# Four feed-forward units of six by seven block products, two of their four weight sums made by accumulating DMA reads

## The reference

```python
D_MODEL, SEQ, D_FF = 1024, 256, 2816

def rmsnorm(x, g):
    return x * rsqrt(mean(x * x, axis=-1) + 1e-6) * g

def swiglu(x, w_gu, w_down):                   # w_gu: 1024 x 5632, w_down: 2816 x 1024
    gate, up = split(x @ w_gu, 2, axis=-1)
    return (silu(gate) * up) @ w_down

for i in range(4):
    x = x + 0.5 * swiglu(rmsnorm(x, ffn1_norm[i]), ffn1_w_gu[i], ffn1_w_down[i])
    x = x + mixer_i(rmsnorm(x, mix_norm[i]))    # attention, SSD, short convolution, attention
    x = x + 0.5 * swiglu(rmsnorm(x, ffn2_norm[i]), ffn2_w_gu[i], ffn2_w_down[i])
```

## Time and profile before

| | |
|---|---|
| median of three runs | 2102.91 us |
| profiled execution | 2101.92 us |
| its span, first to last instruction | 2100.2 us |
| mean granted TensorE clock | 0.995 |
| busy: PE, DVE, ACT, POOL | 98%, 72%, 53%, 4% |
| DMA: bytes moved, mean rate | 369.5 MB, 176 GB/s |
| one feed-forward, from 345.7 to 527.8 us | 182.1 us |

### The profile page before, as it was taken

The page is one execution under the profiler, slowest core; times in us unless marked ns, Lnnn a source line. Parts: engine busy times, 40 slices in busy tenths (PEclk is TensorE's granted clock), DMA queues, the critical chain, the costliest instruction groups (busy, mean ns, idle before and its releaser), DMA issues.

```text
span 2100.2 us, 25376 instructions
## 1 busy us (share of the span) xinstructions
PE 2061.0 (98%) x10493; PEld 1741.3 (83%) x10493; DVE 1503.2 (72%) x1431; ACT 1116.2 (53%) x1180; POOL 79.9 (4%) x110
## 2 busy tenths in 40 slices
PE   7999999999999999999999999999999999999998
PEld 5888887888888789988888888988888888988886
DVE  6885556885976568868776885779758776557884
ACT  5454555554654465655545554446545554556453
POOL 1000000000000002210000000000000000000000
PEclk9999999999999999999999999999999999999999
DMA  5755533655456384454575655565464665523751
GB/s 204 241 200 166 175 101 100 221 195 185 165 176 203 120 262 121 122 198 163 179 242 161 220 188 164 171 200 201 164 229 130 219 228 170 164 81 100 240 201 70
DMA packets 216838, 369.54 MB, mean 176 GB/s; under 512 B 9900, under 2 KB 92164, under 8 KB 216212
## 3 DMA queue, kind: packets, MB, share of 16 engines
q1 hardware_dynamic: 216020, 363.65, 52.5%
q0 software_dynamic: 704, 4.28, 0.5%
HBM read 366.81 MB, written 1.08 MB: 175 GB/s over the span
## 4 chain that ended last, share of the span: by engine, by line
PE 87%; DVE 5%; ACT 4%; POOL 1%; issue 1%; DMA 1%; SPq 0%; POOLq 0%; DVEq 0%; ACTq 0%
PE bank L1424 59%; PE bank L1545 14%; PE bank L1430 7%; ACT w_hi L645 2%; PE bank L1577 2%; DVE w_lo L996 2%; DVE arena L1295 2%; PE bank L1717 1%; PE bank L1709 1%; PE bank L1463 1%; DMA stage<-in_ssd_w_in 1%; POOL yms L579 0%; ACT arena L893 0%; PE bank L1710 0%; PE bank L1718 0%
## 5 line engine op out<-in xcount | busy, mean ns | idle before, releaser
L996 DVE TENSOR_TENSOR w_lo<-stage,w_hi 128x2048 fp32r<-128x2048 f32 (+1 forms) x248 | 560.8, 2264 | 231.5 <-ACT w_hi L645 230.6
L645 ACT ACTIVATE w_hi<-stage 128x2048 fp32r<-128x2048 f32 (+1 forms) x248 | 468.8, 1891 | 309.5 <-PE bank L1424 204.6
L996 DVE TENSOR_TENSOR w_lo<-arena,w_hi 128x2048 fp32r<-128x2048 f32 (+1 forms) x149 | 337.7, 2267 | 146.5 <-ACT w_hi L645 146.5
L1424 PE MATMUL bank<-w_hi,xt_hi 128*128 128x512 f32 (+1 forms) x1040 | 412.4, 397 | 7.1 <-ACT par L764 4.6
L1424 PE MATMUL bank<-w_lo,xt_hi 128*128 128x512 f32 (+1 forms) x1040 | 406.8, 391 | 0.0
L645 ACT ACTIVATE w_hi<-arena 128x2048 fp32r<-128x2048 f32 (+1 forms) x149 | 282.8, 1899 | 188.7 <-PE bank L1424 132.5
L1424 PE MATMUL bank<-w_hi,xt_lo 128*128 128x512 f32 (+1 forms) x1040 | 383.1, 390 | 0.0
L1424 PE MATMUL bank<-w_hi,mt_hi 128*128 128x512 f32 x864 | 341.4, 395 | 1.3 <-DVE mt_lo L1202 1.1
L1424 PE MATMUL bank<-w_hi,mt_lo 128*128 128x512 f32 x864 | 337.3, 390 | 0.0
L1424 PE MATMUL bank<-w_lo,mt_hi 128*128 128x512 f32 x864 | 336.8, 390 | 0.0
L1424 PEld LDWEIGHTS bank<-w_hi,xt_hi 128*128 128x128 f32 x1040 | 198.0, 190 | 50.8 <-issue 10.5
(11 more groups left out here) (191 smaller groups left out, 2345.9 us busy)
## 6 DMA issues: line engine op xcount, KB each, us to landing
stage<-in_ffn_w_gu SPq DMA_DIRECT2D x97, 1024.0 KB, 5.2
arena<-in_ffn_w_gu SPq DMA_DIRECT2D x63, 1024.0 KB, 5.2
stage<-in_ffn_w_down SPq DMA_DIRECT2D x92, 512.0 KB, 4.3
arena<-in_ffn_w_down SPq DMA_DIRECT2D x84, 512.0 KB, 4.3
stage<-in_ffn_w_gu SPq DMA_DIRECT2D x24, 512.0 KB, 4.7
arena<-in_sb_w_qkv SPq DMA_DIRECT2D x16, 512.0 KB, 4.2
stage<-in_sb_w_qkv SPq DMA_DIRECT2D x16, 512.0 KB, 4.4
stage<-in_ssd_w_in SPq DMA_DIRECT2D x8, 1024.0 KB, 5.1
```

The lines of the kernel that those rows point to most:

```text
L645: act.activation(w_hi[q][:, 0:c], stage[s][:, 0:c], ACT.Copy).then_inc(hi_done, 1)
L996: dve.tensor_tensor(w_lo[q][:, 0:c], stage[s][:, 0:c], w_hi[q][:, 0:c].bitcast(F32), ALU.subtract).then_inc(lo_done, 1)
L1424: mm = pe.matmul(out_, x_[a], w[b], start=start and (a, b) == (0, 0), stop=stop and (a, b) == (1, 0))
```

## The change

Units 1 to 4 become units of kind S ("PSSSSH"). The signs are turned so that all four weight sums are additions: A1 = B11 + B12, A3 = B12 + B22, A2 = A1 + B22, A4 = B21 + A2. A1 and A3 are no longer made by DVE: POOL issues DMAs that read the weights of B12 (or B22) from HBM a second time and add them to what lies in the slot of B11 (or B12). POOL issues the one for A1 when `w_lo` of B11 is written, since it overwrites B11's slot. ACT's split of A1 waits for its landing (`a1_in`). Of a unit's two down blocks the first stands in the following unit, the second in the one after that. There are six stage slots instead of five; the SiLU and hidden tiles now lie over `squares`.

```diff
-STAGE_SLOTS = 5
+STAGE_SLOTS = 6
-UNITS = "PSPSPH"
+UNITS = "PSSSSH"
...
+        own = {"P": ("G0", "G1", "U0", "U1"), "H": ("H0", "H1"),
+               "S": ("B11", "A1", "B22", "A3", "B21", "A2", "A4")}[kind]
+        own = [(u, name) for name in own]
+        order += own[:1] + late
+        if u:
+            turned[u - 1] = len(order) - 1
+        order += own[1:2]
+        if u == len(UNITS) - 1:
+            order += own[2:] + down[:1]
+            turned[u] = len(order) - 1
+            order += down[1:] + [(u, f"D{j}") for j in range(down_parts(u))]
         else:
+            order += down[:1] + own[2:]
+            late = down[1:]
...
-LAST_USE = {"B11": "T2", "B12": "T3", "B22": "B21", "B21": "T4"}
-SUM_STEP = {"T1": 1, "T3": 2, "T2": 3, "T4": 4}
+LAST_USE = {"B11": "A2", "B12": "A3", "B22": "A3", "B21": "A4"}
+BY_DMA = 1
+SUM_STEP = {"A2": 1, "A4": 2} if BY_DMA else {"A1": 1, "A3": 2, "A2": 3, "A4": 4}
...
-        sg = area(2 * 512).rearrange("p (h c) -> p h c", h=2)
-        hid = area(2 * 512).rearrange("p (h c) -> p h c", h=2)
+        sg, hid = squares[:, 0:2, :], squares[:, 2:4, :]
...
+            def weight_sums(p):
...
+                for u in range(N_UNITS):
+                    if UNITS[u] != "S":
+                        continue
+                    c0 = DFF + unit_col(u)
+                    (to, _), (other, landed) = home[p, u, "B11"], home[p, u, "B12"]
+                    pool.wait_ge(lo_done, base[p] + FFN_ORDER.index((u, "B11")) + 1)
+                    pool.dma_start(stage[to][:, :].rearrange("p (k c) -> p k c", k=4), rows(w_gu, 0, 4, c0, 512),
+                                   accum_op=ALU.add).then_inc(a1_in, 16)
+                    pool.wait_ge(stage_in[other], landed)
+                    pool.dma_start(stage[other][:, :].rearrange("p (k c) -> p k c", k=4), rows(w_gu, 512, 4, c0, 512),
+                                   accum_op=ALU.add).then_inc(a3_in, 16)
...
             for p in range(n_phases + 1):
                 phase_rstd(p)
+                if p < n_phases and PHASES[p][0] == "ffn":
+                    weight_sums(p)
...
-                if name in HOME:
-                    act.wait_ge(w_summed, 4 * sums_before(nth("ffn", p), u) + SUM_STEP[name])
+                sums = sums_before(nth("ffn", p), u)
+                if name in SUM_STEP:
+                    act.wait_ge(w_summed, len(SUM_STEP) * sums + SUM_STEP[name])
+                elif name == "A1":
+                    act.wait_ge(a1_in, 16 * (sums + 1))
+                elif name == "A3":
+                    act.wait_ge(a3_in, 16 * (sums + 1))
...
-                        if name == "B11":
-                            weight_sum(u, "T1")
-                        elif name == "T3":
-                            weight_sum(u, "T2")
+                        if name == "B11" and not BY_DMA:
+                            weight_sum(u, "A1")
+                        elif name == "A1" and not BY_DMA:
+                            weight_sum(u, "A3")
+                        elif name == "B22":
+                            weight_sum(u, "A2")
                         elif name == "B21":
-                            weight_sum(u, "T4")
+                            weight_sum(u, "A4")
```

More of the change, by code:

```diff
@@ L64, in ffn_order @@
 def ffn_order():
-    order = []
+    order, turned, late = [], {}, []
     for u, kind in enumerate(UNITS):
         down = [(u - 1, f"D{j}") for j in range(down_parts(u - 1))] if u else []
[L69 to L72, removed]
-        else:
-            order += [(u, "B11"), (u, "T1"), (u, "B22")] + down + [(u, "T3"), (u, "B21"), (u, "T2"), (u, "T4")]
-    return order + [(len(UNITS) - 1, f"D{j}") for j in range(down_parts(len(UNITS) - 1))]
+        own = {"P": ("G0", "G1", "U0", "U1"), "H": ("H0", "H1"),
[9 more added lines that the diff above has]
+            order += down[1:] + [(u, f"D{j}") for j in range(down_parts(u))]
+        else:
+            order += down[:1] + own[2:]
+            late = down[1:]
+    return order, turned
+FFN_ORDER, TURNED_AFTER = ffn_order()
 N_UNITS, N_SUMS = len(UNITS), UNITS.count("S")
-FFN_ORDER = ffn_order()
-HOME = {"T1": "B11", "T2": "B11", "T3": "B12", "T4": "B21"}
-LAST_USE = {"B11": "T2", "B12": "T3", "B22": "B21", "B21": "T4"}
-SUM_STEP = {"T1": 1, "T3": 2, "T2": 3, "T4": 4}
+HOME = {"A1": "B11", "A2": "B11", "A3": "B12", "A4": "B21"}
+LAST_USE = {"B11": "A2", "B12": "A3", "B22": "A3", "B21": "A4"}
+BY_DMA = 1
+SUM_STEP = {"A2": 1, "A4": 2} if BY_DMA else {"A1": 1, "A3": 2, "A2": 3, "A4": 4}
 FILLERS = (((0,), (1,)), ((), (2,)), ((), (3,)), ((), (4,)))
@@ L233, in build_trunk @@
             u, name = FFN_ORDER[i]
-            if name == "T1":
+            if name == "B11":
+                slot_of[n], loaded[n] = home[p, u, name] = place(p, i, name, 1)
                 home[p, u, "B12"] = place(p, i, "B12", 1)
+                continue
             if name in HOME:
@@ L441, in hidden_at @@
         def hidden_at(u):
[L443 removed]
+            return 4 * (u % 2)
         def sum_pair(i):
@@ L739, in released @@
                         part(p1, bank[4], i)
-                    elif name == "T1":
+                    elif name == "A1":
                         part(p5, bank[5], i)
-                        hidden_hi(u - 1)
-                    elif name == "T2":
+                    elif name == "A2":
                         part(p16, bank[4], i)
-                    elif name == "D0" and u == N_UNITS - 2:
-                        hidden_hi(u + 1)
+                    for v in range(N_UNITS):
+                        if TURNED_AFTER[v] == i:
+                            hidden_hi(v)
                 def released_by_sums(u, name):
@@ L1617, in ffn @@
                         down(u, int(name[1]), n)
-                    if name in ("G0", "H0", "T1") and u >= 1:
-                        hidden_transpose(u - 1)
-                    elif name == "D0" and u == N_UNITS - 2:
-                        hidden_transpose(u + 1)
+                    for v in range(N_UNITS):
+                        if TURNED_AFTER[v] == i:
+                            hidden_transpose(v)
             def out_part(p, kq, nb, h, ks=range(4)):
```

67 lines of the change are left out of this document (34 added, 33 removed).

## The result

| | before | after |
|---|---|---|
| median | 2104.48 us (4 runs, 2100.06 to 2109.03) | 2345.43 us (4 runs, 2337.53 to 2346.96) |
| profiled execution, its span | 2101.92, 2100.2 us | 2337.53, 2335.4 us |
| mean granted clock | 0.995 | 0.957 |

The ratio is 1.1137 with a 95% interval of 1.1102 to 1.1173. The change makes the kernel 11.4% slower, 241 us, 30.1 us a feed-forward.

A forecast was written before the change was run, and what follows sets the result against it. PE was taken to bound the kernel. Per feed-forward, -5.4 (matmuls) + 5.6 (DVE) + 25.2 (landing stalls) + 4.8 (clock) = +30.2 us; eight, +242 on 2102, gave 2340 us, range 2170 to 2520.

The forecast's parts named there:

- What bounds the kernel: PE, busy 98% of the span, sets the time, fed by splits that are ready early.
- matmuls and crowding: Per feed-forward: 24 fewer matmuls, -5.4 us; DVE falling behind in four S units, 1.4 us each, +5.6 us.
- The chain behind A1: A1's DMA starts after B11's `w_lo`; its late landing delays ACT's queued SiLU and PE's transposes: 25.2 us a feed-forward.
- The landing: A1's DMA: 10.4 us from issue to landing into units 2 to 4, 9.4 into unit 1.
- The second read: The adding DMA also reads what is in the slot, 2.6 us on top of a plain landing of 6.8 us.
- The budgets: Landing time allowed for A1's DMA before a stall: 4.8 us into units 2 to 4, 1.0 into unit 1.
- the signs: Profile after: PE idle 5 to 9 us before transposes, four times a feed-forward; PE waits about a us for `w_lo`.
- The clock: Each of four stalls lowers PE's granted clock, 1.2 us each net of DVE catching up, +4.8 us a feed-forward.
- Slower adding: Rival: each add costs more than a second read, landing 14.7 us, +52.6 us a feed-forward, 2520 us; chance 0.13.
- Short landing: Rival: A1's DMA lands in 4.4 or 6.8 us, kernel at 2131 to 2198 us; chance 0.16.
- POOL slowed by DVE: Rival: DVE's long instructions hold POOL before it issues, 1.3 us on each of 32 A1 landings, 2380 us; chance 0.04.
- Hidden and faster: Rival: A1's landings cause no stall, DVE's 3.6 us are hidden, only saved matmuls count, 2058 us; chance 0.03.

The follow-up runs named there:

- e1: Changed kernel without both adding DMAs of POOL, for A1 and A3, those sums left out: 2115.68 us, ratio 1.0066 to before.
- e8: Changed kernel with UNITS back to "PSPSPH" (two S units), all else of the change kept: 2192.35 us, ratio 1.0412 to before.
- e2: Changed kernel with only A1's DMA left out (its sum left out), A3's kept: 2117.55 us, ratio 1.0067 to before.
- e9: Changed kernel with A1 in its own slot: SP loads B12 there again, POOL adds B11 once that landed: 2124.23 us, ratio 1.0094 to before.
- e4: Changed kernel with ACT doing a unit's second SiLU ahead of the split of the next A1: 2318.10 us, ratio 1.1021 to before.
- e3: Changed kernel with POOL's two DMAs copying instead of adding (sums left out): 2210.72 us, ratio 1.0513 to before.
- e5: Changed kernel with idle matmuls ahead of the transposes, 24 into unit 1, 12 into units 2 to 4: 2305.01 us, ratio 1.0944 to before.

## Why the prediction was right

**What bounds the kernel.** PE at full clock, fed by splits. Right: 192 matmuls went and nothing came back, as DVE is too close. e1 gives that sum by itself: -5.4 + 5.6 = +0.2 a feed-forward was forecast for matmuls and crowding, +1.6 was measured (12.9 us / 8), 1.3 of it inside the feed-forwards. The crowding was taken at 1.4 us for each of four S units and is some 1.65. It was right to count it for all four, though units 1 and 3 had been of kind S before without it; e8 suggests why.

**The chain behind A1.** This was the deciding step and every link of it is in the timeline above: issue 5.8 us after A2's start (5.5 forecast), 3.3 us from landing to product (3.3 forecast). e2 shows that it is this DMA alone, e9 that its start is at fault. The prediction laid the stall on the SiLU in ACT's queue. e4 corrects that: without that queue the wait stands at A1's product, and the time falls by only 27.3 us, 1.1 for each of the 24 stalls.

**The landing.** Forecast 10.4 and 9.4 us, measured 8.8. The plain MB was taken at 6.8, from a DMA of another shape that shared its queue with three others; of the weights, with one more behind it, it is 5.7 (e3). The second read was taken at 2.6 us and is 3.1, with 0.5 of it in the issue. The budgets were too small as well: for unit 4 in the timeline PE takes 14.6 us from A2's start to the transposes, not 13.6, so the budget is 5.5 us, not 4.8; into unit 1 it was 1.0 us on paper and about 8.8 - 6.1 = 2.7 in the trace. So the stalls in front of the transposes are 6.1 + 3 x 3.4 = 16.2 us a feed-forward, not 25.2, and those into units 2 to 4 are under the 5 to 9 us that the prediction named as its sign.

**What was missing.** Behind three of four stalls PE waits once more, up to 1.1 us for `w_lo` of A1 (such waits are 37.4 us against 20.4 in e1, 2.1 a feed-forward more), since ACT's SiLU and DVE's product stand between A1's `w_hi` and its `w_lo`. No term of the sum had it, though the signs named it.

**The clock.** +4.8 was forecast, net of what DVE catches up; filling the pauses gave back 5.0 (e5). Gross it is more: 0.94 over 212.6 us. PE's listed waits are 181.9 us, 22.7 a feed-forward, which less 5.4 of matmuls is 17.3 of the 30.1 us. The other 12.8 are the slow clock (89.9 us more lost than before by the mean clocks, 11.2 a feed-forward, part of it in the pauses) and the tail of a matmul, which the trace counts as busy although it is a pause of 0.16 us at each of the 120 waits (0.39 us of latency at a start every 0.23).

So the total, 30.2 forecast and 30.1 measured a feed-forward, is better than its terms: the landing term was too large by some 9 us, and the second wait, the tails and the gross cost of the clock filled it. That the total came out is partly luck.

**The rivals.** Slower adding: no, 180 GB/s is half of a copy, not less. The Trainium skill's "Collectives: The Full Stack", in its section on the fold count, puts reduce-scatter, which adds, at half the rate of all-gather, which copies, for its two source reads (1.93 measured there). This case's traces agree, 352 to 180 GB/s, a factor of 1.96, though they are of a local add. Short landing: no, 8.8 us. The Trainium skill's fit in "DMA: Bandwidth & Descriptors" (section on the anatomy of one DMA on the gpsimd path) gives an estimate of 4.4 us for 1 MB, which is under the 5.7 us of e3's copies and far under the add's 8.8. POOL slowed by DVE: issues of line 622 took 1274 to 1383 ns throughout, so none was held by the 1.3 us of that rival. Hidden and faster: even with the adds left out the kernel is not faster.

## What to carry to other kernels

An asynchronous operation in place of an engine's frees that engine, but its start is bound to a condition and its end to a consumer. Count the time between the two in the rows of the pace-setting engine and compare it with the landing before asking what it saves. Here the sum in place could start only after the split of B11 and had 5 us for 9; in a slot of its own it starts some 12 us earlier, and the kernel is within 9 us of e1, which has no adding DMA at all. And an engine busy for 86% of a feed-forward (157.0 of 182.8 us in e1) can be at its limit over six short products: take the busy share over the densest stretch, and look at what a new order puts there.

## What was not expected of the hardware

- POOL needs longer to issue an adding DMA: 1.28 us for A1's and 1.84 for A3's right behind it (1.28 where it goes alone, e2), against 0.75 for a copy of the same shape, and such a DMA has almost twice the packets (34496 against 18112 on the queue).
- Over its queue an add has half the rate of a copy, 180 against 352 GB/s.
- A pause of 3.1 us, with another of 1.1 just behind it, was enough to lower the clock here: 0.64 over the next 4.5 us, and 1.00 after that; the two pauses before it, of 3.4 and 3.3 us, were followed by 6.8 us at 0.50. Twelve matmuls in the pause (24 in that into unit 1) kept the clock at 1.00 over the feed-forward of e5.
